# Two-layer decoder trunk with mixture of experts: attention heads' maxima joined, one engine for the probability copies, scores ahead of transposes, and another order of the opening loads and gates

## What is computed

```python
q, k_c, v_c, k_s, v_s, k_w, v_w, gate_logits = jnp.split(h @ w_in, splits, axis=-1)
q = rmsnorm(q.reshape(B, S, H, Dh), q_norm);  q_rot = apply_rope(q, cos, sin)
k_cmp = rmsnorm(compress(kv(k_c), ...), k_norm[0]);  v_cmp = compress(kv(v_c), ...)
gates = jax.nn.sigmoid(gate_logits).reshape(B, S, 3, H)
p_c = masked_softmax(s_c, cmp_end <= t)      # 31 compressed blocks
p_s = masked_softmax(s_s, s_mask)            # selected blocks, rotated q and k_s
p_w = masked_softmax(s_w, w_mask)            # window of 512, rotated q and k_w
o = g0 * (p_c @ v_cmp) + g1 * (p_s @ v_s) + g2 * (p_w @ v_w)
return o.reshape(B, S, NSA_Q_DIM) @ w_out
```

## Time and profile before

| | us |
|---|---|
| median of 3 executions | 1925.23 (1923.52 to 1929.95) |
| profiled execution, its own time | 1925.15 |
| span in the profile, first to last instruction | 1923.4 |
| TensorE matmuls busy | 1500.5 (78%) |
| VectorE / ScalarE / GpSimd busy | 636.3 / 299.5 / 233.7 |
| mean granted TensorE clock | 0.939 of full speed |
| DMA | 468.10 MB, mean 243 GB/s |

### The profile page before, as it was taken

One profiled execution on the slowest core, in us unless ns is written; L12 is line 12 of the kernel. 1 busy time (PEld: TensorE's weight loads), 2 busy tenths in 40 slices (PEclk: granted clock), 3 DMA queues, 4 the chain that ended last, 5 costly groups with the idle time before them and its releaser, 6 DMA issues. The chain is left out here.

```text
span 1923.4 us, 24373 instructions
## 1 busy us (share of the span) xinstructions
PE 1500.5 (78%) x8935; PEld 859.9 (45%) x8935; DVE 636.3 (33%) x1688; ACT 299.5 (16%) x858; POOL 233.7 (12%) x277
## 2 busy tenths in 40 slices
PE   5998889989687777777775687779677777777772
PEld 4554455555443443344343465545444334434431
DVE  3034478863511111111113255542531111111113
ACT  1021245541100000000001222221110000000000
POOL 2011100000211111111113100000111111111112
PEclk7999899999799999999997888979889999999997
DMA  5111110014379999999985300000469999999994
GB/s 232 44 45 66 66 66 2 1 50 170 127 323 429 429 427 420 421 422 417 421 340 188 153 1 0 0 1 21 203 267 429 427 426 421 419 419 422 419 424 174
DMA packets 39412, 468.10 MB, mean 243 GB/s; under 512 B 11680, under 2 KB 12192, under 8 KB 21568
## 3 DMA queue, kind: packets, MB, share of 16 engines
q1 hardware_dynamic: 21424, 433.86, 53.7%
q0 software_dynamic: 15920, 28.45, 4.2%
q10 hardware_dynamic: 2016, 5.10, 0.7%
HBM read 452.66 MB, written 39.85 MB: 256 GB/s over the span
## 5 line engine op out<-in xcount | busy, mean ns | idle before, releaser
L1013 PE MATMUL ps<-sb_ring,sb_x_block 128*64 128x256 f32 x4096 | 471.2, 383 | 170.7 <-DMA sb_ring<-moe_w 166.3
L1013 PEld LDWEIGHTS ps<-sb_ring,sb_x_block 128*64 128x64 f32 x4096 | 311.2, 137 | 382.1 <-issue 146.8
L1022 PE MATMUL ps<-sb_ring,sb_hidT 128*64 128x512 f32 x1024 | 248.0, 605 | 45.5 <-ACT sb_hidT L753 45.5
L1666 DVE COPY sb_row_now<-sb_row_of 128x1 uint32 (+1 forms) x128 | 19.7, 154 | 761.4 <-PE ps L1022 761.4
L660 POOL DMA_INDIRECT expert_rows<-sb_y_sb,sb_row_now x128 | 126.1, 985 | 862.0 <-DVE sb_y_sb L1667 840.0
L753 ACT COPY sb_hidT<-ps 128x128 f32<-128x128 f32 x128 | 34.1, 266 | 886.4 <-PE ps L1082 886.4
L1022 PEld LDWEIGHTS ps<-sb_ring,sb_hidT 128*64 128x64 f32 x1024 | 62.1, 136 | 143.0 <-issue 73.1
L1667 DVE COPY sb_y_sb<-ps 128x512 f32<-128x512 f32 x128 | 87.0, 680 | 0.0
L938 ACT ACTIVATE sb_ring<-ps,sb_n_max_of 128x128 f32<-128x128 f32 (+3 forms) x128 | 66.4, 524 | 83.4 <-DVE sb_n_max_of L2008 83.4
L1456 PE MATMUL ps<-sb_ident,sb_ring 128*128 128x128 f32 x320 | 52.1, 296 | 23.5 <-DVE sb_ring L2038 21.5
L1676 DVE COPY sb_x_block<-sb_xsT 128x512 f32 x132 | 56.4, 427 | 24.6 <-issue 22.5
(11 more groups left out here) (279 smaller groups left out, 1635.1 us busy)
## 6 DMA issues: line engine op xcount, KB each, us to landing
sb_ring<-moe_w SPq DMA_DIRECT2D x128, 3072.0 KB, 16.4
sb_xsT<-nsa_w_group SPq DMA_DIRECT2D x2, 2048.0 KB, 17.5
sb_ring<-nsa_w_group SPq DMA_DIRECT2D x2, 2048.0 KB, 7.6
sb_xsT<-nsa_w_out SPq DMA_DIRECT2D x1, 4096.0 KB, 12.0
token_rows<-sb_h_norm ACTq DMA_DIRECT2D x8, 512.0 KB, 3.2
sb_ring<-mla_w_out SPq DMA_DIRECT2D x1, 4096.0 KB, 12.1
sb_ring<-mla_w_in SPq DMA_DIRECT2D x1, 2304.0 KB, 8.1
sb_x_res<-x SPq DMA_DIRECT2D x4, 512.0 KB, 7.2
```

Source lines behind the costliest of these rows:

```text
L1013: last = nc.tensor.matmul(ps[j * BLOCK:(j + 1) * BLOCK, bank, 0:2 * P].rearrange("p (g n) -> p g n", g=2), x_rows[:, k, :], weights[:, 0:2 ...
L1022: last = nc.tensor.matmul(ps[j * BLOCK:(j + 1) * BLOCK, 2, :], hidT[:, c * BLOCK:(c + 1) * BLOCK], weights[:, 2, c * D + j * 512:c * D + ( ...
```

## The change

In the opening, `gain` of the first norm is issued by ScalarE ahead of all else, and the six small loads by SP behind `w_kv`. GpSimd issues no load before its constants; `mla_gain` and the router loads go behind the first unit's scales. The gates are no longer formed tile by tile: behind the four groups TensorE forms them in one piece as 48 rows by 512 tokens (eight products), ScalarE exponentiates that, and behind unit 0's products four small transposes turn it back (`turn_gates`); VectorE adds one and takes the reciprocal behind unit 0's rotation. In the attention loop one maximum instruction covers both heads, and so does one reciprocal; `exps` waits for the joined maximum, `scale_probs` for both exponentials; all copies to `n_probsT` are ScalarE's; and `scores(s+2)` stands ahead of `turn_probs(s)`. Some semaphores are merged, which moves no instruction.

```diff
 
             def nsa_loads():
                 sp.dma_start(w_kv, a["nsa_w_kv"]).then_inc(kv_loaded, 16)
+                for name, tile in (("nsa_w_gates", w_gates), ("nsa_cmp_pos", kc_T[:, KV_GROUPS, 0:CMP_LEN]),
+                                   ("rope", turn[:, :, :, :]), ("cmp_mask", cmp_mask), ("nsa_cmp_w2", cmp_w2)):
+                    sp.dma_start(tile, a[name]).then_inc(nsa_small, 16)
+                sp.dma_start(nsa_gain.rearrange("p r d -> p (r d)"), a["nsa_gain"].partition_broadcast(P)).then_inc(nsa_small, 16)
                 sp.dma_start(cmp_w1, a["nsa_cmp_w1"]).then_inc(cmp_loaded, 16)
                 sp.dma_start(w_even, a["nsa_w_group"][0]).then_inc(even_loaded, 16)
...
                 pool.dma_start(gain[:, :], g[ph // 2:ph // 2 + 1, :].partition_broadcast(P)
                                ).then_inc(gain_loaded, 16)
 
-            gains(stages[0])
+            norms[0] += 1
             step(pool.memset(ones[:, :], 1.0))
...
                 pool.dma_start(b_router[:, :], a["moe_b_router"][l:l + 1, :].partition_broadcast(P)).then_inc(router_loaded, 16)
                 pool.dma_start(router_gain[:, :], a["norm_ffn"][l:l + 1, :].rearrange("o (p k) -> (o p) k", k=KD)).then_inc(router_loaded, 16)
 
-            pool.dma_start(mla_gain[:, :], a["mla_gain"].partition_broadcast(P)).then_inc(small_loaded, 16)
-            if 1 in stages:
-                load_router(0)
-
             def unit_scales(u):
 
...
             def nsa_scales():
                 for u in range(UNITS):
                     unit_scales(u)
+                    if u == 0:
+                        pool.dma_start(mla_gain[:, :], a["mla_gain"].partition_broadcast(P)).then_inc(small_loaded, 16)
+                        load_router(0)
...
                 turn_output()
 
             def nsa_act():
-                for name, tile in (("rope", turn[:, :, :, :]), ("cmp_mask", cmp_mask), ("nsa_w_gates", w_gates),
-                                   ("nsa_cmp_w2", cmp_w2), ("nsa_cmp_pos", kc_T[:, KV_GROUPS, 0:CMP_LEN])):
-                    act.dma_start(tile, a[name]).then_inc(nsa_small, 16)
-                act.dma_start(nsa_gain.rearrange("p r d -> p (r d)"), a["nsa_gain"].partition_broadcast(P)).then_inc(nsa_small, 16)
+                act.dma_start(gain[:, :], a["norm_mix"][0:1, :].partition_broadcast(P)).then_inc(first_gain, 16)
                 norm_squares()
 
-                act.wait_ge(gates_done, 1)
-                nc.scalar.activation(gates, ps[:, 4, 0:TILES * GATES].rearrange("p (t n) -> p t n", t=TILES),
-                                     ACT.Exp, scale=-1.0).then_inc(gates_exp, 1)
                 for g in range(KV_GROUPS):
                     act.wait_ge(kv_done, g + 1)
                     nc.scalar.copy(kc_T[:, g, :], ps[:, 5 + g % 3, :]).then_inc(kv_taken, 1)
+                act.wait_ge(gates_done, 1)
+                nc.scalar.activation(gates_T[0:GATES, :], ps[0:GATES, 3, :], ACT.Exp, scale=-1.0).then_inc(gates_exp, 1)
 
                 def unit_rows(u):
...
                 def exps(s):
                     n = (s % TILES + 1) * P
                     for r in range(2):
-                        act.wait_ge(n_max, 2 * s + r + 1)
+                        act.wait_ge(n_max, s + 1)
                         if s >= 4:
 
                             act.wait_ge(n_turned, 2 * (s - 4) + r + 1)
@@ -942,12 +938,11 @@
                 exps(0)
                 exps(1)
                 for s in range(ATTEND):
-                    if s % 2:
-                        n = (s % TILES + 1) * P
-                        act.wait_ge(n_turned, 2 * s + 2)
-                        if s >= 2:
-                            act.wait_ge(n_weighed, s - 1)
-                        nc.scalar.copy(n_probsT[:, s % 2, :, 0:n], ps[:, 4:6, 0:n]).then_inc(nT_ready, 1)
+                    n = (s % TILES + 1) * P
+                    act.wait_ge(n_turned, 2 * s + 2)
+                    if s >= 2:
+                        act.wait_ge(n_weighed, s - 1)
+                    nc.scalar.copy(n_probsT[:, s % 2, :, 0:n], ps[:, 4:6, 0:n]).then_inc(nT_ready, 1)
                     if s == 4:
                         unit_columns(UNITS - 1, 0)
...
             def nsa_pe():
                 mm = nc.tensor.matmul
 
-                def gate_logits(t):
-                    if t == 0:
-                        pe.wait_ge(nsa_small, NSA_SMALL)
-                    for k in range(KD):
-                        last = mm(ps[:, 4, t * GATES:(t + 1) * GATES], hT[:, k, t * P:(t + 1) * P], w_gates[:, k, :],
-                                  start=(k == 0), stop=(k == KD - 1))
-                    if t == TILES - 1:
-                        last.then_inc(gates_done, 1)
-
-                turn_rows(h, gate_logits)
+                turn_rows(h)
                 pe.wait_ge(kv_loaded, 16)
                 for g in range(KV_GROUPS):
                     if g == 3:
@@ -1318,6 +1304,17 @@
                         last = mm(ps[:, 5 + g % 3, :], w_kv[:, k, g * 2 * DH:(g + 1) * 2 * DH], hT[:, k, :],
                                   start=(k == 0), stop=(k == KD - 1))
                     last.then_inc(kv_done, 1)
+                pe.wait_ge(nsa_small, NSA_SMALL)
+                for k in range(KD):
+                    last = mm(ps[0:GATES, 3, :], w_gates[:, k, :], hT[:, k, :], start=(k == 0), stop=(k == KD - 1))
+                last.then_inc(gates_done, 1)
+
+                def turn_gates():
+                    pe.wait_ge(gates_exp, 1)
+                    for t in range(TILES):
+                        last = nc.tensor.transpose(ps[:, 2, t * GATES:(t + 1) * GATES], gates_T[0:GATES, t * P:(t + 1) * P],
+                                                   ident[0:GATES, 0:GATES])
+                    last.then_inc(gates_turned, 1)
 
                 def unit_rows(u, ks):
...
                     if part == 0:
                         pe.wait_ge(u_rotated, 2 * u + 2)
                         pe.wait_ge(u_normed, u + 1)
+                        if u == 1:
+                            pe.wait_ge(gates_ready, 1)
                         if 2 <= u < UNITS - 1:
...
                         unit_columns(u - 2, 1)
                     unit_rows(u, range(KD // 2, KD))
                     if u == 0:
+                        turn_gates()
                         pack()
                     if u == 1:
...
                 unit_columns(UNITS - 2, 1)
                 scores(1)
                 for s in range(ATTEND + 1):
+                    if s + 2 < ATTEND:
+                        scores(s + 2)
                     if s < ATTEND:
                         turn_probs(s)
-                    if s + 2 < ATTEND:
-                        scores(s + 2)
                     if s >= 1:
                         weigh(s - 1)
...
                 step.mark(v.tensor_tensor(cos_t, spread(turn[:, 0], 0, DH), gains_of(0, DH), ALU.mult))
                 step.mark(v.tensor_tensor(sin_t[:, :, :, 0:half], spread(turn[:, 1], 0, half), gains_of(half, DH), ALU.mult))
                 step(v.tensor_tensor(sin_t[:, :, :, half:DH], spread(turn[:, 1], half, DH), gains_of(0, half), ALU.mult))
-                dve.wait_ge(gates_exp, 1)
-                step(v.tensor_scalar(gates, gates, 1.0, None, ALU.add))
-                step(v.reciprocal(gates, gates))
-
                 def unit_sums(u):
                     dve.wait_ge(u_squared, u + 1)
...
                     unit_sums(u)
                     unit_norm(u)
                     unit_rotate(u)
+                    if u == 0:
+                        dve.wait_ge(gates_turned, 1)
+                        step(v.tensor_scalar(gates, ps[:, 2, 0:TILES * GATES].rearrange("p (t n) -> p t n", t=TILES), 1.0, None, ALU.add))
+                        v.reciprocal(gates, gates).then_inc(gates_ready, 1)
                     if u == 1:
                         sum_keys()
...
                 def top(s):
                     n = (s % TILES + 1) * P
                     dve.wait_ge(n_scored, s + 1)
-                    for r in range(2):
-                        v.tensor_reduce(n_max_of[:, s % 4, r:r + 1], ps[:, score_bank(s) + r, 0:n], AX, ALU.max,
-                                        negate=True).then_inc(n_max, 1)
+                    v.tensor_reduce(n_max_of[:, s % 4, :], ps[:, score_bank(s):score_bank(s) + 2, 0:n], AX, ALU.max,
+                                    negate=True).then_inc(n_max, 1)
 
                 def scale_probs(s):
                     pair, kind, t = s // PAIR_STEPS, s // TILES % 2, s % TILES
                     n = (t + 1) * P
+                    dve.wait_ge(n_exp, 2 * s + 2)
+                    step(v.reciprocal(n_weight[:, s % 4, :], n_sum_of[:, s % 4, :]))
                     for r in range(2):
                         column = (1 + kind) * NSA_HEADS + 2 * pair + r
-                        dve.wait_ge(n_exp, 2 * s + r + 1)
-                        step(v.reciprocal(n_weight[:, s % 4, r:r + 1], n_sum_of[:, s % 4, r:r + 1]))
```

(7 more changed lines are left out.)

78 lines of the change are left out of this document (38 added, 40 removed).

## The result

The changed kernel takes **1911.04 us** (median of 10 runs, 1902.39 to 1916.41) against 1925.40 (10 runs in the same job, 1919.85 to 1929.95): ratio 0.9928, 95% interval 0.9912 to 0.9944, so 14 us or 0.7% faster. The profiled execution took 1915.49 us with a span of 1913.7.

The account below looks back on a forecast made before the run. Bounds: in the opening, TensorE's wait for small loads and gate work delaying projections; in the attention loop, a VectorE-ScalarE ring. Opening -17.8 plus loop +3.5 is -14.3 us, from 1925.2 to 1910.9 us; 8-in-10 range 1901 to 1923.

Parts of the forecast that it names:

- the opening: Start of kernel to first units: projections start 25.2 us sooner, 6.9 and 0.5 given back for gates, -17.8 us in all.
- the steady rounds: Attention loop: eleven new rounds of 11.83 us take 130.1 us against 123.9, so +6.3 us.
- the low stretches: Attention loop: 2 us added for new stretches with TensorE at its lower clock level.
- the end of the loop: Attention loop after its last steady rounds: +0.6 us.
- I put tile 0 three microseconds earlier: Opening: first tile of h ready 3 us sooner, so tile 3 near 15.8 and projections start at 18.5 us.
- the 52 to 56 that I had called right: Opening: sign that the forecast is right, units starting at 52 to 56 us (72.70 before).
- The ring: Attention loop: VectorE and ScalarE wait on each other in turn; joins end head overlap, round 11.83 us against 10.99.
- The first four rounds: Attention loop's start: 51.6 us against 56.96, keeping 4.3 of 13.0 us extra, so -5.4 us.
- The second rival: Attention loop: TensorE's lower clock level in each of 16 rounds, costing 12 us, not 2; 1921 us in all; chance 0.17.
- The loop, +3.5: Whole attention loop: +6.3 + 0.6 - 5.4 + 2 = +3.5 us, bounds -3 and +14.
- Rival one: Attention loop: VectorE's occupancy decides, TensorE's 9.9 us bound the round, -23 us in the loop, 1884 us total; chance 0.07.
- Rival three: Attention loop: TensorE falls to its lower clock level and stays, +5.5 us a round, up to 1977 us; chance 0.05.

Follow-up runs that it names:

- gain_pool: Changed kernel with the first gain fetched by GpSimd at the head of its stream again, not by ScalarE: 1909.56 us.
- opening_alone: Changed kernel with all four attention-loop edits undone (maxima and reciprocals per head, copies shared, transposes first), so only the opening is new: 1908.14 us.
- turn_first: Changed kernel with TensorE's transposes of step s ahead of the scores of s+2 again: 1912.36 us.
- loop_alone: Kernel before, with only the four attention-loop edits: 1927.97 us, 2.0 above the kernel before in its job.
- maxima_first: Changed kernel, joins kept, but on VectorE the joined maximum of step s+2 stands ahead of the scalings of s+1: 1878.64 us.
- heads_apart: Changed kernel with maxima and reciprocals per head again; copies stay on ScalarE and scores stay ahead of transposes: 1877.45 us.

## Why the prediction was right, and where it was off

The time, 1910.9 against 1911.04, is nearer than the steps deserve. Up to the end of the loop the profiled execution leads by 13.9 us where the sum has 14.3, with four terms off by 1 to 2 us: the opening by +2.0, the steady rounds by -1.1, the low stretches by -1.9, the end of the loop by +1.5. That they cancel is luck, and so is the last 0.1 us: the ten runs lie between 1902.39 and 1916.41, and the profiled one took 1915.49. The mechanism, a gain in the opening less a small loss in a ring made longer by the joins, held.

- **Opening, -17.8: measured -15.8** at the first exponential in the profiled execution. "I put tile 0 three microseconds earlier" failed: it came 1.76 us earlier, and tile 3's chain then ended at 19.80 in place of 18.5 (+1.3). With the gain's load issued beside x, the first square came at 6.17 us, later than before (5.27); gain_pool, where GpSimd issues it at 1.33, has it at 4.18. The gates cost 7.07 us, as said (6.9). The projections took 29.66 us and not 29.0 (+0.6). That last term is the clock's, not the edit's: where TensorE was at its upper level from 15 us on (opening_alone) the same 32 products (64 records) took 27.70, and there the units started at 54.4 us, the very start that the sum gives (43.68 to 18.5, then 6.9 more); here they started at 56.40, just behind the 52 to 56 that I had called right. By medians the opening is worth 17.8 us. One reading was loose, though the sum did not use it: TensorE's idle time of 11.54 us began at 15.28 (26.82 - 11.54), before the last tile was scaled at 18.71, and not behind it.
- **The ring: right step by step.** Predicted 2.30, 2.92, 3.53, 3.08; measured 2.28, 2.89, 3.51, 3.05. The round is 11.73 where 11.83 was said, eleven of them (266.74 to 395.91) 129.2 where 130.1 was said. The price of a joined maximum (0.42 and 1.22) was right to 1%.
- **The first four rounds: 51.5 us, 51.6 predicted**, though the choice to keep 4.3 of 13.0 us was the softest step.
- **The end of the loop, +0.6: measured +2.1** (17.0 us from the last round's start to the projection, 14.9 before). The term left out the last eight transposes at the lower level (1.94 us) behind a wait of 2.35 for both scalings, with nothing beside them.
- **New low stretches, +2: under 0.2 us.** Two of the eleven steady rounds had their eight transposes at the lower level (1.92 and 1.83 us) and lengthened by 0.14 and 0. The second rival did not happen: the lower level came in two rounds and not in all, and the slack of the scores, which it reckoned as half of the cost, took nearly all of it.
- **The loop, +3.5: +1.9** in the profiled execution, +2.0 by the medians of loop_alone, +2.9 by the medians of changed and opening_alone.

Rival one (1884 us, "if the next step's maxima can be started earlier than I think") did not happen, for the reason given: "VectorE's program order, scaling, maxima, scaling, leaves no way around". maxima_first changes just that order and gets 1878.64. The work on TensorE was put too high there. The 9.9 us a round are right for the old order (39.72 us busy in the four rounds from 299.03 of the kernel before), but the prediction carried them over to the new one, in which they are 9.3: it had no term for what scores ahead of transposes save on TensorE itself. In the changed kernel, where TensorE is not the bound, that cost nothing. Rival three did not happen.

The rule of the Trainium skill ("VectorE: DVE Perf Modes", section on the TRN2 errata) that one large tile beats several small ones is right for the engine's time: VectorE is busy 600.8 us in the changed kernel and 614.9 in heads_apart, which differs by the joins alone. (The 636.3 of before has the copies in it too.) The section speaks of operands in SBUF; the joined maxima read `ps`, and there two of 0.280 us against one of 0.417 agree. It says nothing of who waits for the first part of the result, and here that decided. Where the order gives the joined form room it holds for the time too: 9.62 against 9.84 us a round with maxima first. The rule of the Trainium skill on transposes ("TensorE: Matmul & The Clock Gate", Part 4: PE-mode transpose) is neither borne out nor refuted: in heads_apart such transposes are 31% of TensorE's busy time between 300 and 350 us (15.4 of 49.63), and each of its rounds from the fifth on takes 9.33 to 9.41 us, the upper level throughout; but other products stand between them.

## What to carry to other kernels

Before joining the instructions of two independent streams, draw the ring they are in: a join that saves an engine's time lengthens every chain that could have gone on with the first half, here by 2.3 us a round, for 0.9 us of VectorE's busy time saved (614.9 less 600.8 us, in 16 rounds). Where the join is wanted, first reorder so that its result is not the last thing the other engine waits for; that was worth as much as undoing it (32 us against 34). Look at the order of an engine's work also where nothing waits: scores ahead of transposes took 0.6 us a round off TensorE's own time, which showed only once TensorE was the bound. And a change that moves the time by little may hold parts that cancel: test the parts, not the sum.

## What was not expected

- The same 32 products (64 records) took 27.70, 29.66 and 30.13 us in kernels whose streams are alike up to there (opening_alone, changed, turn_first), by when TensorE's clock rose. Between 20 and 25 us opening_alone gets 13 of the records, the changed kernel 8 and turn_first 7. The windows' clock says 1.00, 0.62 and 1.00 for these: where durations and this column differ, I went by the durations. TensorE's work before was the same, with starts within 0.1 us, so I have no cause for it.
- Equal rounds of the changed kernel got different levels: the eight transposes of t = 3 took 1.92 us at 324.97 and 1.83 at 371.78, and 1.06 or 1.07 in the rounds between.
- Which engine issues the gain moved the landings of x (squares at 4.18 and 6.17 us) and of the gain (8.4 and 6.4) by 2.0 us each in opposite directions, and the gain's first use not at all (8.45 and 8.43).
